# Order of the work in the mixer of a hybrid encoder step: indexer, k and v first, then scores and q, then the convolution, with the top-k selection beside them

## The reference

```python
h = rms_norm(x, g_norm_mix) * (1 + sc_a) + sh_a              # adaLN, sc/sh/gate from silu(c) @ w_ada
q, k, v, iq, ik, iw, u = jnp.split(h @ w_in, SPLIT_POINTS, axis=-1)   # 512,128,128,512,64,8,1024 columns
q, k = rope(rms_norm(q)), rope(rms_norm(k)); iq, ik = rope(iq), rope(ik)
g = a * jax.nn.sigmoid(b)                                    # a, b = the halves of u
# indexer: one score for each query and key, over 8 heads
dots  = jnp.einsum('bqhd,bsd->bqhs', qi, ik_all)
score = jnp.einsum('bqhs,bqh->bqs', jax.nn.relu(dots), wi)
top_val, top_idx = lax.top_k(where(admissible, score, -inf), k_top)
# attention of q over the chosen keys only (8 heads, 2 KV heads), softmax
# convolution: causal depthwise, 31 taps, over concat(state, g); LayerNorm over 512 channels; silu
x = x + gate * (concat(attention, conv) @ w_out)
```

## Time and profile before

| | before |
|---|---|
| three runs | 1506.32, 1513.5, 1505.99 us |
| the profiled execution | 1509.73 us, span 1507.9 us |
| mixer of layer 0, from u's first matmul to the output projection | 47.57 to 432.47 us |
| mixer of layer 1, the same | 798.62 to 1168.61 us |
| PE, DVE, ACT, POOL busy in the span | 1251.6, 546.0, 376.0, 143.2 us |

### The profile page before, as it was taken

The page is one execution under the profiler, slowest core; times in us unless marked ns, Lnnn a source line. Parts: engine busy times, 40 slices in busy tenths (PEclk is TensorE's granted clock), DMA queues, the critical chain, the costliest instruction groups (busy, mean ns, idle before and its releaser), DMA issues. The chain is left out here.

```text
span 1507.9 us, 16186 instructions
## 1 busy us (share of the span) xinstructions
PE 1251.6 (83%) x6299; PEld 740.3 (49%) x6299; DVE 546.0 (36%) x1394; ACT 376.0 (25%) x842; POOL 143.2 (9%) x216
## 2 busy tenths in 40 slices
PE   3999998945899879999709999888477995999980
PEld 0554444422445466777405545453245454777750
DVE  2100058848525521111051000589583454111114
ACT  2100142145631111111131001511558111111112
POOL 0400000340000150000021000004200011000002
PEclk7999999965999879999959999979558996999995
DMA  9524167299860589999581231111002026699975
GB/s 359 162 61 117 57 220 262 91 398 312 292 230 29 183 287 364 365 362 368 181 295 35 62 79 56 64 64 56 8 23 55 1 86 214 231 367 362 364 251 188
DMA packets 137126, 284.99 MB, mean 189 GB/s; under 512 B 11565, under 2 KB 91861, under 8 KB 130649
## 3 DMA queue, kind: packets, MB, share of 16 engines
q1 hardware_dynamic: 116416, 209.70, 41.3%
q0 software_dynamic: 8352, 42.50, 8.2%
q10 hardware_dynamic: 12281, 31.74, 5.9%
HBM read 237.91 MB, written 52.40 MB: 193 GB/s over the span
## 5 line engine op out<-in xcount | busy, mean ns | idle before, releaser
L470 PE MATMUL ps<-W,arena 128*128 128x256 f32 (+1 forms) x1280 | 347.4, 427 | 8.4 <-ACT arena L1188 2.8
L470 PEld LDWEIGHTS ps<-W,arena 128*128 128x128 f32 x1280 | 241.8, 193 | 84.2 <-issue 54.3
L480 PE MATMUL ps<-C,arena 128*128 128x128 f32 (+3 forms) x851 | 128.0, 296 | 85.2 <-ACT arena L1063 17.2
L470 PE MATMUL ps<-W,hT 128*128 128x512 f32 (+5 forms) x640 | 193.9, 464 | 1.3 <-DVE gt L1265 1.3
L480 PEld LDWEIGHTS ps<-C,arena 128*128 128x128 f32 (+3 forms) x851 | 104.4, 157 | 120.0 <-issue 54.3
L470 PEld LDWEIGHTS ps<-W,hT 128*128 128x128 f32 (+1 forms) x640 | 103.2, 182 | 90.3 <-issue 81.0
L749 PE MATMUL ps<-W,hT 128*128 128x512 f32 (+1 forms) x320 | 142.1, 597 | 1.0 <-issue 1.0
L470 PE MATMUL ps<-hT,W 128*128 128x64 f32 (+1 forms) x512 | 140.1, 434 | 2.6 <-ACT hT L927 2.6
L470 PEld LDWEIGHTS ps<-hT,W 128*128 128x128 f32 x512 | 77.8, 191 | 64.5 <-issue 61.2
L749 PEld LDWEIGHTS ps<-W,hT 128*128 128x128 f32 (+1 forms) x320 | 56.2, 181 | 73.6 <-issue 73.5
L1653 DVE TENSOR_TENSOR arena<-arena,ps 128x256 f32<-128x256 f32 x32 | 13.5, 421 | 216.2 <-ACT arena L1180 216.2
(11 more groups left out here) (244 smaller groups left out, 1130.4 us busy)
## 6 DMA issues: line engine op xcount, KB each, us to landing
W<-in_w_ada SPq DMA_DIRECT2D x48, 1024.0 KB, 7.1
W<-in_w_gate SPq DMA_DIRECT2D x32, 1024.0 KB, 10.6
W<-in_w_up SPq DMA_DIRECT2D x32, 1024.0 KB, 13.0
W<-in_w_down SPq DMA_DIRECT2D x32, 1024.0 KB, 7.8
arena<-x_d SPq DMA_DIRECT2D x33, 512.0 KB, 10.7
y_d<-arena ACTq DMA_DIRECT2D x33, 512.0 KB, 7.2
W<-in_w_in SPq DMA_DIRECT2D x16, 1024.0 KB, 15.4
arena<-arena SPq DMA_DIRECT2D x128, 79.2 KB, 2.1
```

The source lines that it names most:

```text
L470: ins = T.matmul(out, l, r, start=n == 0, stop=n == len(pairs) - 1, skip_group_check=True)
L480: count(T.transpose(o, i, ident[0:m, 0:m]), done if n == len(outs_ins) - 1 else None)
```

## The change

The mixer's stages are put in another order on every engine.

- PE: iq, ik, then k and v; then transposes and the 32 dots. In layer 1 one of the five q projections (`project_q`) follows each four dots; in layer 0 the 16 adaLN steps stay with the dots and the q projections follow them. Then u and the convolution, in layer 0 with the next eight adaLN steps (`ada3`) between. The means `lnm` and variances `lnv` of the LayerNorm stand just in front of the attention.
- DVE: `select(rounds)` takes rounds from one list `left` over tiles 4, 3, 2, 1. Behind each four scores it does 2 rounds (layer 0) or 3 (layer 1); layer 0 does 3 more beside each q projection; the rest goes in four pieces in front of the four gate products. The attention holds no selection.
- ACT: relu, squares and roots of q in groups of four; the LayerNorm's root after group 7's work and its silu behind the ten groups, in front of the last `outputs`. Before the first relu it now waits until the indexer k outputs have been stored (`outst` 32), since `sq` has moved onto their memory.
- POOL: the tap matrices 2 and 3 come behind q's rotary; the square for the variance is a POOL multiply, no longer an ACT activation; the 16 MB of filling DMAs go out at the end of layer 0's dots.
- SP: the loads follow PE's new order, and `shifted` goes with them.

```diff
-        sq = part(0, 3200, NT, 10, HD)
+        sq = part(2544, 640, NT, 2, HD)
+        sqq = part(2544, 512, 8, HD)
-        lnb = part(20312, 576)
+        lnb = part(8704, 576)
-        AB = [part(17336, 2048, 2, D), part(10880, 2048, 2, D)]
+        AB = [part(15168, 2048, 2, D), part(10880, 2048, 2, D)]
-        gf = part(15168, 1024)
+        gf = part(5120, 1024)
...
                 for c in range(8):
+                    if l == 0 and c == 3:
+                        ada(U_ADA1, 0)
...
-                    if c == 3:
-                        shifted(0)
...
-                            w, c0, c1 = {2: (win, CIQ, CIK), 3: (win, CIK, CU), 4: (win, CK, CIQ), 5: (win, CQ, CK),
+                            w, c0, c1 = {0: (win, CIQ, CIK), 1: (win, CIK, CU), 2: (win, CK, CIQ), 3: (win, CQ, CK),
...
-                    if c == 3:
+                    if l == 0 and c == 4:
+                        ada(ada3_use(0), 2, range(2))
+                    if l == 0 and c == 5:
+                        shifted(0)
+                        ada(ada3_use(2) - 2, 2, range(2, 6))
                         shifted(1)
                         shifted(2)
-                    if c == 4 and l == 1:
+                        ada(ada3_use(2) - 2, 2, range(6, KC))
                         shifted(3)
+                        ada(U_ADA4, 3)
+                        ada(U_ADA5, 4)
+                    if l == 1 and c == 6:
+                        for i in range(4):
+                            shifted(i)
...
+                for n, (c, w) in enumerate(((0, 512), (1, 72), (2, 256))):
+                    for t in range(NT):
+                        project(c, w, 5 * n + t, t, t == 0, t == NT - 1)
+
+                pe.wait_ge(L["tapc"], 1)
                 pe.wait_ge(L["ropei"], 2)
+                for i in range(5):
+                    turn([(ps[3 + i][:, t * P:(t + 1) * P], iqf[:, t, i * P:(i + 1) * P]) for t in range(4)], L["tr"])
...
+                def project_q(n):
+                    project(3, 512, 15 + n, ATTN[n], n == 0, n == NT - 1)
-                    if n == 8:
-                        pe.wait_ge(L["lnsq"], 1)
-                        products(ps[2][:, 0:SEQ], [(ones, sqc[:, c, 0:SEQ]) for c in range(4)], L["lnv"])
-                        products(ps[0][:, 0:DEC], [(ones, sqc[:, c, SEQ:TOK]) for c in range(4)], L["lnv"])
...
                     if l == 0 and n % 2 == 1:
                         third, k = divmod(n // 2, KC)
                         if k == 0:
-                            pe.wait_ge(*((L["lnx"], 1), (L["lnr"], 1))[third])
+                            pe.wait_ge(L["proja"], 15)
                         ada(ps[1 - third], (U_ADA1, U_ADA2)[third], [k], third)
+                    if l == 1 and n % 4 == 3 and 1 <= n // 4 <= 5:
+                        project_q(n // 4 - 1)
+                    for n in range(NT):
+                        project_q(n)
...
+                def u_block(i):
+
+                    c = 4 + i // 2
+                    pe.wait_ge(*((s_glu, 4 * l + i - 1) if i >= 2 else (L["rel"], 32)))
+                        if i >= 1 and smp and ab == 0:
+                            pe.wait_ge(s_glu, 4 * l + i)
...
+                def conv(i):
+                    pe.wait_ge(s_g4[i % 2], (2 * l + i // 2 + 1) * 256)
+                    pe.wait_ge(L["w4"], i + 1)
+                    pe.wait_ge(*((L["cyd"], i) if i >= 1 else (L["proja"], 20)))
...
+                u_block(0)
+                ada3(0)
+                u_block(1)
+                ada3(1)
+                conv(0)
+                u_block(2)
+                ada3(2, 3)
+                conv(1)
+                u_block(3)
+                ada3(4, 5)
+                conv(2)
+                ada3(6)
+
+                pe.wait_ge(s_glu, 4 * l + 4)
+                turn([(ps[5][0:30, c * P:(c + 1) * P], gT[:, c, 512:542]) for c in range(4)], L["cst"])
+                turn([(ps[6][0:30, c * P:(c + 1) * P], gT[:, c, 606:636]) for c in range(4)], L["cst"])
+                turn([(ps[3][:, c * P:(c + 1) * P], ck[:, c]) for c in range(4)], L["tq"])
+                pe.wait_ge(L["ropeq"], 2)
+                turn([(ps[4][:, t * P:(t + 1) * P], qkf[:, t, 512:640]) for t in range(4)], L["tq"])
+                turn([(ps[7][:, 0:DEC], qkf[0:DEC, 4, 512:640])], L["tq"])
+                conv(3)
+                ada3(7)
                 for n in range(4):
                     turn_q(n)
+                pe.wait_ge(L["cyd"], 4)
+                pe.wait_ge(L["tqa"], 5)
+                products(ps[5][:, 0:SEQ], [(ones, cy[:, c, 0:SEQ]) for c in range(4)], L["lnm"])
+                products(ps[6][:, 0:DEC], [(ones, cy[:, c, SEQ:TOK]) for c in range(4)], L["lnm"])
...
                 logits(0)
                 turn_q(4)
                 logits(1)
                 pe.wait_ge(L["tqa"], 8)
+                pe.wait_ge(L["lnsq"], 1)
+                products(ps[6][:, 0:SEQ], [(ones, sqc[:, c, 0:SEQ]) for c in range(4)], L["lnv"])
+                products(ps[3][:, 0:DEC], [(ones, sqc[:, c, SEQ:TOK]) for c in range(4)], L["lnv"])
+                pe.wait_ge(L["lnr"], 1)
...
...
+                act.wait_ge(L["outst"], 32)
+                act.wait_ge(L["proja"], 15)
+                for r, t0, t1 in PARTS:
+                    S.activation(sq[0:r, t0:t1], qkr[0:r, t0:t1, KH, :], ACT.Square).then_inc(L["qsq"], 1)
+                store("new_v_prompt", tiles, vrow[:, 0:4, :])
+                store("new_v_sample", row, vrow[0:DEC, 4, :])
...
+                    if n % 4 < 3:
+                        continue
+                    g = n // 4
+                    if g == 0:
+                        sqrt_qk(2, PARTS, KH)
+                    if l == 1 and 1 <= g <= 5:
+                        q_squares(g - 1)
+                    if l == 1 and 2 <= g <= 5:
+                        q_root(g - 2)
+                    if l == 1 and g == 7:
+                        q_root(4)
+                    if l == 0 and g == 6:
                         keep_mod(0)
...
+                    for n in range(NT):
+                        q_squares(n)
+                        q_root(n)
...
-                act.wait_ge(L["lny"], 1)
-                for c in range(4):
-                    S.activation(hT[:, 4 + c, :], cy[:, c, :], ACT.Silu, bias=vT[:, 48 + c:49 + c],
-                                 scale=vT[:, 44 + c:45 + c]).then_inc(L["mixy"], 1)
...
+                    if n == 7:
+                        act.wait_ge(L["lnr"], 1)
+                        S.activation(lnb[:, :], lnb[:, :], ACT.Sqrt).then_inc(L["lnr"], 1)
                     if n == 3:
-
-                        act.wait_ge(L["mixy"], 4)
+                        act.wait_ge(L["lnr"], 1)
...
+                act.wait_ge(L["lny"], 1)
+                for c in range(4):
+                    S.activation(hT[:, 4 + c, :], cy[:, c, :], ACT.Silu, bias=vT[:, 48 + c:49 + c],
+                                 scale=vT[:, 44 + c:45 + c]).then_inc(L["mixy"], 1)
                 outputs(9)
...
+                left = [(t, r) for t in SCORED for r in range(TOPK[t] // 8)]
+
+                def select(rounds):
+
+                    for _ in range(min(rounds, len(left))):
+                        t, r = left.pop(0)
+                        m, n = rows_of(t), NKEYS[t]
+                        sc = msk[0:m, MSK_AT[t]:MSK_AT[t] + n]
+                        m8 = small[0:m, S_M8:S_M8 + 8]
+                        if t < 4 and r == 0:
+                            chain(V.memset(sc[0:64, n - 64:n], -BIG))
+                        chain(V.max(m8, sc))
+                        chain(V.match_replace(sc, m8, sc, MARK))
+                        if r == TOPK[t] // 8 - 1:
+                            chain(V.tensor_scalar(sc, sc, MARK, -BIG, ALU.not_equal, ALU.mult))
...
+                    if n % 4 < 3:
+                        continue
+                    g = n // 4
+                    if g == 0:
+                        reduced(PARTS, KH, [sq[0:r, t0:t1] for r, t0, t1 in PARTS], 2)
+                    if g == 1:
+                        dve.wait_ge(L["score"], 8)
+                        inverted(PARTS, KH, 1)
+                    if l == 1 and 2 <= g <= 6:
+                        q_reduced(g - 2)
+                    if l == 1 and g >= 3:
+                        q_inverted(g - 3)
+                    if g >= 1:
+                        select(3 if l == 1 else 2)
...
-                select(4, 0, 0.75)
-                reduced(PARTS, KH, 2)
-                select(4, 0.75, 1)
-                inverted(PARTS, KH, 1)
-                q_reduced(0)
-                select(3, 0, 0.25)
...
+                    for n in range(NT):
+                        q_reduced(n)
+                        select(3)
+                        q_inverted(n)
+                for i, rounds in enumerate((10, 12, 18, 100)):
+                    select(rounds)
+                    dve.wait_ge(L["sig"], i + 1)
+                    at = P * (i % 2)
```

(27 more changed lines are left out.)

387 lines of the change are left out of this document (140 added, 247 removed).

## The result

The changed kernel takes 1491.13 us (median of four runs, 1488.32 to 1492.59) against 1509.91 for the kernel before: ratio 0.9877, 95% interval 0.9856 to 0.9898, so 1.2% faster. The 1509.91 is the median of four runs (a fourth of 1514.01 us has joined the three listed). I had forecast 1487, which is 19 us less than the median of those three; the difference measured is 18.8. The profiled execution took 1492.04 us with a span of 1490.2.

What follows compares the result with a forecast made beforehand. PE was taken to bound the kernel; layer 1's terms made -19.5 us and layer 0's -2.2, together -22, less 3 kept for unseen waits, about -19 from the median: 1487 us. The range holding 8 in 10 was 1468 to 1507.

Steps and rivals of the forecast that it cites:

- Start of the dots: ACT's new work before the first relu makes DVE's first score later: +2.5 us in each layer (bounds 1.5 and 5).
- Dots and q, layer 0: Layer 0's dots at 54 us against 45.9, q projections +1.5 for clock: net +9.5 us (bounds +3 and +20).
- over 90% busy: Sign expected in the profile after: DVE busy over 90% in both layers' dot stages.
- Dots and q, layer 1: Interleaved stage about 65 us against 75.8, less +5 for clock: net -6 us (bounds -12 and +15).
- u and convolution: First three convolutions hidden; conv(3) waits for gate, product, issues and landing: +3.5 us in layer 1, +0.3 in layer 0.
- In front of the attention: Stretch before the attention becomes a chain of 25.5 us: -9.5 us in layer 1, -5.5 in layer 0.
- Attention: Without selection long waits go, less +4 for root and silu tail: -10 us layer 1, -9 layer 0 (bounds -20 and 0).
- they cancel except where a wait or a clock changes: PE's projections, convolutions, turns, adaLN steps and products keep number and shape, so they were left out of the cost.
- (a): Rival: DVE beside the dots is the only loss and the clock holds; 15 us more gain, 1472 us; chance 0.24.
- (b): Rival: layer 0's dots cost 12 us more, attention gives only 5 a layer; 1508 us, no measurable change; chance 0.16.
- (c): Rival: PE at 1.2 GHz in layer 1's q projections between dots, 7 us per low projection; 1527 us; chance 0.10.
- (d): Rival: DVE's late first gate product stalls conv(0) and each following convolution, 2 to 3 us a stage, within the range.

Runs made afterwards that it cites:

- Experiment 9: Changed kernel; squares of k and q in other memory, last turned q copied before first exponentials, output projection's attention half started while silu runs: 1482.24 us, ratio 0.9822.
- Experiment 3: Changed kernel without the selection rounds beside the dots (14 in layer 0, 21 in layer 1): 1511.59 us, ratio 1.0016.
- experiment 7: Changed kernel with the LayerNorm's square in front of the attention on ACT instead of GpSimd: 1496.56 us, ratio 0.9911.
- experiment 1: Kernel before the change, without the 32 selection rounds inside each layer's attention: 1490.4 us, ratio 0.9883.
- experiment 2: Kernel before, without the attention's selection, and with the four fills issued at the end of layer 0's dots: 1519.73 us, one run.
- experiment 5: Changed kernel with the fills behind the centring: 1504.85 us; also with rounds beside layer 0's dots and layer 1's two last groups moved to the convolution: 1484.29 us.

## Why the prediction was right, and where it was not

- **Start of the dots, +2.5.** Right in kind: ACT waited 3.06 us for the indexer store in layer 0 and 0.89 in layer 1, where I had 0 to 1. Experiment 9 took back 4.5 us in layer 0 and 0.2 in layer 1.
- **Dots and q, layer 0, +9.5 beside the start.** 56.5 + 36.2 us against 45.9 + 35.0 for the same projections at full clock makes +11.8, forecast +12 with the start. Experiment 3 shows DVE's rounds as the cause (42.7 us without them). The sign "over 90% busy" did not show for the whole stage (44.57 of 56.5 us), but it did where the rounds stand: up to 129.1 us DVE still waits for the first tile's relus, behind that it is busy 93% of the time:

```profile
112.70:129.10 16.40, 13.76 (x72) 3.54 (x76) 7.39 (x13) 6.40 (x21) 0.00 (x0) 0.79 0.68 236
129.10:169.10 40.00, 28.84 (x140) 7.13 (x135) 37.15 (x70) 11.40 (x24) 9.41 (x20) 0.78 0.97 349
```

- **Dots and q, layer 1, -6 with +2.5 at the start.** Measured 71.0 against 75.8, -4.8 for -3.5 forecast. But the forecast held up to 5 us for low clock behind thin work, at the first q projection and at u, and u's share of it, 2.7, falls into the next stage: so -2.1 for -3.5. The first q projection took 9.07 us against 7.1 for the others. The bound is PE's cycle of 10 us, and DVE (52.85 of 71.0 us busy) only in the two last groups.
- **u and convolution, +3.5 in layer 1.** This is the term of layer 1 that was mis-sized most. Against layer 0, whose stage of 110.8 us holds 6.3 of adaLN steps and a wait of 1.42, layer 1's 113.0 has 8.5 more: 2.7 for the wait (4.14 against 1.42), 2.7 for u's first blocks and 2.8 for conv(3). The last two are PE at half clock behind an idle stretch. I had counted such a loss after the dots but not after conv(3)'s own wait. Measured 4.14 + 2.7 + 2.8 = 9.6 for 3.5, or 6.9 without the 2.7 that the sum had put with the dots.
- **In front of the attention, -9.5 and -5.5.** Layer 1: 22.8 us, and 2.1 of turns that went ahead of conv(3), 24.9 for 25.5 (35.3 less 25.5 is 9.8, which I had put down as 9.5). From the centring's end to the transposes it took 13.3, not 10 to 12, although the square took 4.03 us and not 4.4: DVE's small step was held behind GpSimd's multiply (experiment 7), and the last copy of q stood behind the exponentials (experiment 9).
- **Attention, -10 and -9.** Layer 1: -7.8. Selection itself was worth 15.4 (experiment 1), and 7.6 came back. Compared with experiment 1, PE idles 20.3 us instead of 17.5, with 3.67 behind the root and 2.69 for silu, and is busy 64.6 us instead of 59.8 with the same matmuls, at a lower clock; why it is lower was not tested. The tail was forecast at 4. Layer 0: -13.7, the other mis-sized term. The selection gave 7.0 there and the fills' move another 7 (experiments 1 and 2), which my sum did not contain. In the changed kernel the fills behind the centring cost 10.8 (experiment 5), so the two pieces don't simply add.
- **What the terms leave.** Layer 1's terms as measured make -2.1 + 6.9 - 10.4 - 7.8 = -13.4, and its mixer fell by 10.9. Of the 2.5 between them 1.7 stand in the projections that now open the mixer, 67.4 us for what takes layer 0 65.7; four of the experiments' profiles have 65.8 there in layer 1 too, so this comes and goes without an edit.
- **The step that failed** in layer 0 is thus the sentence that everything else cancels: "they cancel except where a wait or a clock changes". The fills in POOL's queue were moved too, out of the attention and beside q and u, 16.8 MB of DMA that the sum put at nothing. In layer 1 it is the same sentence's clock: 2.8 us behind conv(3)'s wait and 4.8 in the attention were not in the sum.
- **Rivals.** (a) The clock did not hold: 0.62 in layer 1's attention. (b) did not come: layer 0's dots lost as much as forecast and not 12 more, and the attentions gave 13.7 and 7.8, not 5 each. (c) No q projection of layer 1 ran low throughout: PE's clock was 0.90 in that stage, and four of the five projections took 7.1 us. (d) The first gate product did not stall conv(0). Both mixers stayed inside the bounds that I had set for a wrong forecast (-8.2 and -10.9), layer 1's barely: 10 was the bound.

## What to carry to other kernels

When stages change places, list what every queue issues in them, the bulk transfers first: here 16.8 MB decided whether an earlier finish was a gain or a wait for weights. Hide long work of a second engine beside the stage where PE is dense, not where it waits for that engine already. And price a wait of a few us on PE with the matmuls behind it at half clock: here 4.14 us of waiting cost 2.8 more.

## What the hardware showed unexpectedly

- Beside the fills ACT's issue of a broadcast load took 3.66 us instead of 0.46 (experiment 5, DMA share 0.98), and small stores landed so late that ACT waited 44.70 us (experiment 2, share 0.94 in the wait). An issue is then not free: ACT's computing stood still behind two of them.
- A DVE tensor_scalar on 4 columns lasted until GpSimd's multiply of 2304 columns ended (2.70 us instead of 0.17), while DVE's scale, mask and maximum steps, which read PSUM, ran beside the same multiply at 0.28. By the Trainium skill ("SBUF — State Buffer", section "Who interferes with whom") DVE in a 2-port mode and GpSimd take one shared pair of ports for a whole instruction, and the other one blocks; the trace agrees, with the 0.05 us between the two ends. It does not show which mode the step ran in.
